# K and V pages loaded in runs of two rows into every second partition, and the sample softmax spread over several slots

## The reference

```python
def fox_sample(q, k, v, logf, k_past, v_past, logf_past):
    d_new = lax.cumsum(logf, axis=1).transpose(0, 2, 1)
    rev = (lax.cumsum(logf_past, axis=1, reverse=True) - logf_past).transpose(0, 2, 1)
    sp = jnp.einsum('bqhd,bkhd->bhqk', q, k_past) * scale
    sp = sp + d_new[:, :, :, None] + rev[:, :, None, :]
    ...
    p = jax.nn.softmax(jnp.concatenate([sp, sn], axis=-1), axis=-1)
    out = (jnp.einsum('bhqk,bkhd->bqhd', p[..., :n_past], v_past)
           + jnp.einsum('bhqk,bkhd->bqhd', p[..., n_past:], v))
```

## Time and profile before

| | |
|---|---|
| Median of 3 runs | 2012.65 us (2010.44 to 2016.42) |
| The profiled execution's own time | 2018.6 us |
| Its span, first to last instruction | 2016.9 us |
| Mean granted TensorE clock | 0.977 |
| PE, DVE, ACT, POOL busy over the span | 93%, 43%, 22%, 12% |
| Moved by DMA | 458.57 MB, 227 GB/s over the span |
| The slot loop | from about 70 us to 545 us |
| Idle time of POOL before `vpage` issues, ended by PE (L1290) | 233.6 us, 43 times |
| First matmul of the next stage (L1338) | 547.2 us |

### The profile page before, as it was taken

One profiled execution on the slowest core, in us unless ns is written; L12 is line 12 of the kernel. 1 busy time (PEld: TensorE's weight loads), 2 busy tenths in 40 slices (PEclk: granted clock), 3 DMA queues, 4 the chain that ended last, 5 costly groups with the idle time before them and its releaser, 6 DMA issues.

```text
span 2016.9 us, 33708 instructions
## 1 busy us (share of the span) xinstructions
PE 1876.5 (93%) x12473; PEld 1121.2 (56%) x12473; DVE 861.9 (43%) x1921; ACT 440.3 (22%) x1017; POOL 249.4 (12%) x381
## 2 busy tenths in 40 slices
PE   6999998888999999999999998987999999999994
PEld 4677655555488868888874487444333333333331
DVE  5644467777656523333344647245111111111115
ACT  3111124444301011101110305131222222212213
POOL 0203333333100000000000000000111111111110
PEclk9999999999999999999999999996999999999997
DMA  7859999999911140210121205344999999999966
GB/s 255 277 169 343 354 337 364 352 339 347 331 63 65 44 154 11 63 53 11 55 74 63 87 1 183 121 171 177 372 381 382 374 373 376 371 372 374 371 222 264
DMA packets 208164, 458.57 MB, mean 227 GB/s; under 512 B 18721, under 2 KB 47418, under 8 KB 207618
## 3 DMA queue, kind: packets, MB, share of 16 engines
q1 hardware_dynamic: 177554, 365.30, 50.8%
q0 software_dynamic: 30448, 91.13, 12.8%
HBM read 432.44 MB, written 32.17 MB: 230 GB/s over the span
## 4 chain that ended last, share of the span: by engine, by line
PE 82%; DVE 6%; ACT 4%; DMA 4%; issue 3%; DVEq 1%; SPq 0%; ACTq 0%; POOLq 0%; POOL 0%
PE ps L1338 20%; PE ps L1691 11%; PE ps L1722 6%; PE ps L1167 6%; PE ps L1403 6%; PE ps L1702 6%; PE ps L1432 5%; PE ps L1731 3%; PE ps L1182 3%; PE ps L1544 2%; PE ps L1290 2%; PE ps L1270 2%; PE ps L1148 1%; DVE kt L2230 1%; DMA vpage<-in_cache_v 1%
## 5 line engine op out<-in xcount | busy, mean ns | idle before, releaser
L1691 PE MATMUL ps<-gu,xgT 128*64 128x512 f32 x1024 | 228.7, 599 | 0.6 <-ACT xgT L2046 0.6
L1338 PE MATMUL ps<-xnT,ring 128*128 128x264 f32 x768 | 184.5, 392 | 3.2 <-ACT xnT L741 1.9
L2230 DVE STREAM_TRANSPOSE kt<-kraw 128x1024 f32<-128x1024 f32 x128 | 151.1, 1219 | 34.5 <-DMA kraw<-in_cache_k 25.3
L1338 PEld LDWEIGHTS ps<-xnT,ring 128*128 128x128 f32 x768 | 147.8, 193 | 30.5 <-ACT xnT L741 2.2
L876 POOL DMA_DIRECT2D vpage<-in_cache_v x228 | 122.4, 537 | 291.6 <-PE ps L1290 233.6
L3053 DVE TENSOR_TENSOR sig_a<-ps,sig_a 128x256 f32<-128x256 f32 x32 | 13.6, 425 | 322.9 <-ACT sig_a L2050 322.9
L1691 PEld LDWEIGHTS ps<-gu,xgT 128*64 128x64 f32 x1024 | 71.1, 138 | 133.0 <-issue 130.2
L1722 PE MATMUL ps<-wd,hidT_a 128*64 128x512 f32 x512 | 116.9, 598 | 20.2 <-ACT hidT_a L2056 11.2
L1702 PE MATMUL ps<-gu,xgT 128*32 128x512 f32 x1024 | 115.8, 592 | 0.0
L1167 PE MATMUL ps<-xnT,early 128*128 128x352 f32 x320 | 101.2, 472 | 4.4 <-DVE xnT L2174 4.4
L1167 PEld LDWEIGHTS ps<-xnT,early 128*128 128x128 f32 x320 | 60.6, 194 | 38.2 <-issue 8.7
(11 more groups left out here) (482 smaller groups left out, 2945.9 us busy)
## 6 DMA issues: line engine op xcount, KB each, us to landing
kraw<-in_cache_k SPq DMA_DIRECT2D x256, 256.0 KB, 5.3
wd<-in_w_expert_down SPq DMA_DIRECT2D x31, 2048.0 KB, 21.5
gu<-in_w_expert_gate SPq DMA_DIRECT2D x30, 2048.0 KB, 20.3
gu<-in_w_expert_up SPq DMA_DIRECT2D x30, 2048.0 KB, 25.1
vpage<-in_cache_v POOLq DMA_DIRECT2D x228, 256.0 KB, 5.8
ring<-in_w_in SPq DMA_DIRECT2D x12, 1024.0 KB, 8.1
yy<-y_d SPq DMA_DIRECT2D x16, 512.0 KB, 10.4
early<-in_w_in SPq DMA_DIRECT2D x6, 1024.0 KB, 11.7
```

The source lines that it names most:

```text
L1338: last = nc.tensor.matmul(bank(R.bank(name, f, q))[:, 0:QT], weight[:, k], src[:, k, cols], start=k == 0, stop=k == HK - 1)
L1691: last = nc.tensor.matmul(bank(0)[h * BA:(h + 1) * BA, :].rearrange("p (x n) -> p x n", x=2), src[:, k, 0:BA], weight[:, k, :, h * DE // 2 ...
L2230: nc.vector.transpose(kt[n % 2].rearrange("p c e s -> p (c e s)")[:, x * 1024:(x + 1) * 1024], kraw[n % 2].rearrange("p c d -> p (c d)")[: ...
```

## The change

- **Layout of a page.** Page p of a unit goes into the partitions of parity p % 2, two neighbouring rows of 512 floats to a partition (`page_rows`, `page_pairs`): 64 runs of 4 KB in place of 128 runs of 2 KB, for keys and values alike. The position of a token in a unit changes with it, so the order of `rev` changes too: partition p of `past` now holds pages 2p and 2p + 1, DVE writes the sum into a tile `paired` in the new order with four instructions in place of two, PE needs five small matmuls for `later` in place of two, and POOL stores `rev_d` in four DMAs of 64-float runs, without the wait behind them.
- **Joined maxima.** They move out of `join_scores` into `join_tops`, behind the prompt's pieces of the same slot.
- **Exponentials.** The first half of a sample is taken in slots with n % 8 = 0, the second half and the new tokens one slot later.
- **Turned probabilities.** Half a sample is turned in slots with n % 8 = 1 and the other half in slots with n % 8 = 3, both behind `turn_keys`; `st_ready` counts halves, and the load into place 5 waits for 16 of them. The first half waits for the values of the sample before only up to its fourth unit.
- **Queries.** `spread_queries` moves to slots with n % 8 = 4.

```diff
@@ -87,7 +87,7 @@
     c[:, C_ID:C_ID + P] = np.eye(P)
     c[:, C_CAUSAL:C_CAUSAL + P] = np.where(r[None, :] <= r[:, None], 0.0, NEG)
     c[:, C_BEFORE:C_BEFORE + P] = r[:, None] < r[None, :]
-    g, j = r // PAGES, r % PAGES
+    g, j = r // (PAGES // 2), r % (PAGES // 2)
     c[:, C_PAGES:C_PAGES + P] = (g[:, None] == g[None, :]) & (j[:, None] > j[None, :])
     hq, s = np.arange(QH), np.arange(NS)
     own = (s[None, None, :] // DS == np.arange(DB)[None, :, None]) & (s[None, None, :] % DS <= (hq % DS)[:, None, None])
@@ -241,6 +241,7 @@
         past = at("past", [P, 2, PAGE * H], w + 3 * 4096)
         after = at("after", [P, 2, H, PAGE], w + 5 * 4096)
+        paired = at("paired", [P, H, 4, 2, 16, 2], w)
         ptot = at("ptot", [P, 2, H], w + 7 * 4096)
         pgi = at("pgi", [P, 2], w + 7 * 4096 + 64, I32)
         early = [at(f"early{s}", [P, KD, 256], a_ring + s * 8192) for s in range(2)]
@@ -866,20 +867,27 @@
             elif place == 4:
                 R.read(eng, "sp", NSU - 1)
             elif place == 5:
-                eng.wait_ge(st_ready, DB)
+                eng.wait_ge(st_ready, 2 * DB)
+
+        def page_rows(place, p):
+
+            return place[p % 2::2, p // 2 * 2:p // 2 * 2 + 2, :]
+
+        def page_pairs(cache, page):
+
+            return cache[ds(page, 1)].rearrange("a (s j) d -> (a s) j d", j=2)
         def load_values(eng, n):
             numbers = unit_pages(eng, n)
             values_free(eng, n)
             for p, page in enumerate(numbers):
-                eng.dma_start(vpage[value_place(n)][:, p, :], t["cache_v"][ds(page, 1)].rearrange("a s d -> (a s) d")
+                eng.dma_start(page_rows(vpage[value_place(n)], p), page_pairs(t["cache_v"], page)
                               ).then_inc(v_in[value_place(n)], 16)
         def load_keys(eng, n, p, page):
-            eng.dma_start(kraw[n % 2][:, p, :], t["cache_k"][ds(page, 1)].rearrange("a s d -> (a s) d")
-                          ).then_inc(k_in[n % 2], 16)
+            eng.dma_start(page_rows(kraw[n % 2], p), page_pairs(t["cache_k"], page)).then_inc(k_in[n % 2], 16)
         def joined(i):
@@ -916,7 +924,7 @@
             with nc.allow_non_contiguous_dma("page numbers, one per partition"):
-                sp.dma_start(pgi, t["pages"].rearrange("a (g p) -> p (a g)", g=2)).then_inc(tables_in, 16)
+                sp.dma_start(pgi, t["pages"].rearrange("a (p g) -> p (a g)", g=2)).then_inc(tables_in, 16)
             sp.dma_start(convp, t["convp"]).then_inc(tables_in, 16)
@@ -958,7 +966,7 @@
                 load_unit(n)
                 if n == 3:
-                    sp.wait_ge(rev_stored, 16 * 8)
+                    sp.wait_ge(rev_stored, 16 * 4)
                     load_rev(0)
                 if n % SU == 6 and n < (DB - 1) * SU:
@@ -1193,8 +1201,13 @@
                     for g in range(2):
                         R.pe_free(pe, "later", g)
-                        nc.tensor.matmul(bank(R.bank("later", g))[:, 0:H], consts[:, C_PAGES:C_PAGES + P], ptot[:, g, :],
-                                         start=True, stop=True).then_inc(R.full, 1)
+                        for x in range(2):
+                            last = nc.tensor.matmul(bank(R.bank("later", g))[:, 0:H], consts[:, C_PAGES:C_PAGES + P],
+                                                    ptot[:, x, :], start=x == 0, stop=x == 1 and g == 1)
+                        if g == 0:
+                            last = nc.tensor.matmul(bank(R.bank("later", g))[:, 0:H], ident, ptot[:, 1, :],
+                                                    start=False, stop=True)
+                        last.then_inc(R.full, 1)
                 for x in MIX_TURNS[f]:
                     n_mix.pe_turn(pe, x)
             pe.wait_ge(early_k_in, 32)
@@ -1283,7 +1296,7 @@
                 pe.wait_ge(v_in[value_place(n)], 64 * values_in(n) + 64)
-                pe.wait_ge(st_ready, b + 1)
+                pe.wait_ge(st_ready, 2 * b + 1 + u // (SU // 2))
@@ -1885,13 +1898,14 @@
                     copy(("pt", k, p, g), probT[p][:, j0:j0 + nj, :],
                          lambda b: b[:, 0:nj * P].rearrange("p (j x) -> p j x", j=nj))
-            def exp_pages(b):
+            def exp_pages(b, r):
                 act.wait_ge(s_max, b + 1)
+                x = sprob[b % 2][:, r * 512:(r + 1) * 512]
+                nc.scalar.activation(x, x, ACT.Exp, bias=negmax[:, b:b + 1], accum_out=sums[:, b, r:r + 1]
+                                     ).then_inc(s_exp, 1)
+
+            def exp_new(b):
                 act.wait_ge(side_ready, SNEW_READY)
-                for r in range(2):
-                    x = sprob[b % 2][:, r * 512:(r + 1) * 512]
-                    nc.scalar.activation(x, x, ACT.Exp, bias=negmax[:, b:b + 1], accum_out=sums[:, b, r:r + 1]
-                                         ).then_inc(s_exp, 1)
                 nc.scalar.activation(pnew[b % 2], snew[:, b, :], ACT.Exp, bias=negmax[0:QH, b:b + 1],
                                      accum_out=sums[0:QH, b, 2:3]).then_inc(s_exp, 1)
@@ -1921,7 +1935,9 @@
                 if SU <= n < NSU + SU and n % SU == 0:
-                    exp_pages(n // SU - 1)
+                    exp_pages(n // SU - 1, 0)
+                if SU <= n < NSU + SU and n % SU == 1:
+                    exp_pages(n // SU - 1, 1), exp_new(n // SU - 1)
@@ -2205,8 +2221,11 @@
             for g in range(2):
                 R.made(dve, "later", g)
-                nc.vector.tensor_tensor(after[:, g], after[:, g], bank(R.bank("later", g))[:, 0:H].unsqueeze(2)
-                                        .to_broadcast([P, H, PAGE]), ALU.add)
+                for odd in range(2):
+                    nc.vector.tensor_tensor(paired[:, :, :, odd, :, g],
+                                            after[:, g].rearrange("p h (x s o) -> p h x s o", o=2, s=16)[:, :, :, :, odd],
+                                            bank(R.bank("later", g))[:, 0:H].unsqueeze(2).unsqueeze(3)
@@ -2345,23 +2364,27 @@
-                if u == SU - 1:
-                    dve.drain()
-                    for g in range(4):
-                        nc.vector.tensor_reduce(crest[:, g:g + 1], tops[g * QH:(g + 1) * QH, b, :], AX, ALU.max)
-                    dve.drain()
-                    for g in range(4):
-                        last = nc.vector.tensor_reduce(negmax[g * QH:(g + 1) * QH, b:b + 1], crest, AX, ALU.max, negate=True)
-                    last.then_inc(s_max, 1)
-
-            def turn_sample_probs(b):
-
-                dve.wait_ge(s_exp, 3 * b + 3)
+
+            def join_tops(b):
+
+                dve.drain()
+                for g in range(4):
+                    nc.vector.tensor_reduce(crest[:, g:g + 1], tops[g * QH:(g + 1) * QH, b, :], AX, ALU.max)
+                dve.drain()
+                for g in range(4):
+                    last = nc.vector.tensor_reduce(negmax[g * QH:(g + 1) * QH, b:b + 1], crest, AX, ALU.max, negate=True)
+                last.then_inc(s_max, 1)
+
+            def turn_sample_probs(b, r):
+
+                dve.wait_ge(s_exp, 3 * b + (1, 3)[r])
                 if b:
-                    dve.wait_ge(v_used, b * SU)
-                flat = sprobT.rearrange("p u x -> p (u x)")
-                nc.vector.transpose(flat, sprob[b % 2])
-                nc.vector.transpose(pnewT[b % 2], pnew[b % 2]).then_inc(st_ready, 1)
+                    dve.wait_ge(v_used, b * SU - (SU // 2, 0)[r])
+                half = slice(r * 512, (r + 1) * 512)
+                last = nc.vector.transpose(sprobT.rearrange("p u x -> p (u x)")[:, half], sprob[b % 2][:, half])
+                if r == 1:
+                    last = nc.vector.transpose(pnewT[b % 2], pnew[b % 2])
+                last.then_inc(st_ready, 1)
             def mask_own(b):
@@ -2375,8 +2398,6 @@
             for n in range(NSU + LAG):
                 if 0 < n <= NSU:
                     join_scores(n - 1)
-                if n % SU == 0 and n + SU < NSU:
-                    spread_queries(n // SU + 1)
                 if n == PROMPT0 - 1:
                     biased(0, 0)
                 if n == END:
@@ -2392,9 +2413,15 @@
                         invert_sums(k)
                 if n == 5:
                     take_new()
+                if 0 < n <= NSU and n % SU == 0:
+                    join_tops(n // SU - 1)
+                turn_keys(n + 2)
                 if SU < n < NSU + SU and n % SU == 1:
-                    turn_sample_probs(n // SU - 1)
-                turn_keys(n + 2)
+                    turn_sample_probs(n // SU - 1, 0)
+                if SU < n < NSU + SU and n % SU == 3:
+                    turn_sample_probs(n // SU - 1, 1)
+                if n % SU == 4 and n + SU < NSU:
+                    spread_queries(n // SU + 1)
                 if 2 * SU < n < NSU + LAG - 1 and n % SU == 1:
                     mask_own(n // SU - 2)
             near, far = slice(0, HT), slice(HT, NT)
@@ -3151,11 +3178,9 @@
```

(8 more changed lines are left out.)

1 line of the change is left out of this document (added).

## The result

| | before | after |
|---|---|---|
| Median, same chip | 2015.04 us (16 runs, 2009.81 to 2019.90) | 2022.14 us (16 runs, 2018.99 to 2033.83) |
| Ratio | | 1.0046, 95% interval 1.0034 to 1.0058 |
| Profiled execution: span, granted clock | 2016.9 us, 0.977 | 2031.4 us, 0.970 |
| First L1338 (after: L1351) | 547.21 us | 561.38 us |
| From L1294 (L1307) of the seventh sample to it | 29.7 us | 38.2 us |

A forecast was written before the change was run, and what follows sets the result against it. The prediction took the loop as bound by whichever of nearly full PE and DMA engines comes last in a slot. Terms -8.9, -6, -2, -3, +3, +0.9 sum to -16, taking median 2012.65 to 1997 us, range 1978 to 2010.

The forecast's parts named there:

- Rival 1 (DMA was the real bound): Slot loop: the DMA engines are the real bound; -31 us, or 1981 us; chance 0.20.
- Pages, -8.9: Slot loop: 4 KB runs end PE's direct waits on values and keys, -8.9 us, bounds -18.5 and 0.
- the price per piece: Page DMAs in the loop: 87.4 ns per 2 KB piece, 159.7 per 4 KB, so 18.5 us less of all engines.
- Rival 2: Slot loop: the 4 KB runs bring nothing, ends of samples give -8; -5 us, or 2007.5 us; chance 0.15.
- Rival 3 (dearer pieces): Pages in 64 partitions: new pieces cost more, deciding from 183 ns; +7 us, or 2020 us; chance 0.09.
- Maxima and exponentials, -6: Five sample ends: PE's 8.8 us of waits for turned prompt probabilities shrink, -6 us, bounds -8.8 and 0.
- a sign of being wrong: Slot loop: a new wait of ACT for the joined maxima would show the forecast wrong; no size given.
- Diagonal, -2: Slot loop: PE's 7.2 us of waits for the row sums' diagonal fall by 2 us, between 0 and -7.2.
- Clock, -3: Sample ends: shorter gaps bring back some of 8.1 us lost to low clock, -3 us, between 0 and -8.1.
- The end of the loop, +3 (0 to +9): Last half sample turned in slot 67, not 65, so place 5's load comes later; +3 us, 0 to +9.
- Start, +0.9: Before the slot loop: five small matmuls in place of two, without cover on PE, +0.9 us.
- rivals 2 and 4: In 4, the end of the loop eats the gain, +9 there; no change, 2012.6 us; chance 0.06.

The follow-up runs named there:

- Half pages: Kernel before, keys of units 2 to 63 and values of units 2 to 53 loading only rows 0 to 63 of each page: 2011.59 us, ratio 0.9985.
- layout only: Kernel before with the 4 KB page layout, new order of the sums and four rev_d stores alone: 2017.53 us, ratio 1.0016.
- the whole spread: Kernel before with the change's maxima, exponentials, turned probabilities and queries, old pages; with the last sample as before: 2013.52 us, ratio 0.9992.
- DVE's moves alone: Kernel before with only the maxima joined later and the queries spread in slots with n % 8 = 4: 2014.76 us, ratio 1.0006.
- The halves alone: Kernel before with only exponentials and turned probabilities in halves, keys ahead of them, last sample as before: 2010.45 us, ratio 0.9980.
- the two with the halves alone: Kernel before with exponentials and turned probabilities in halves, last sample as before: with old pages 2010.45 us (0.9980), with the 4 KB page layout 2008.68 us (0.9971).
- the spread alone: Kernel before with all of the change but the page layout and order of sums: 2021.54 us (1.0034); with the last sample whole 2013.52 us (0.9992).
- after, the same two ways: The changed kernel as it is, 2022.14 us (1.0046), and with the last sample's exponentials and turned probabilities whole as before, 2017.20 us (1.0012).

## Why the prediction was wrong

- **What bounds the kernel.** I wrote that the loop is bound by whichever comes last and then let the share of 0.98 argue for a DMA bound beside it. Half pages, with 36% fewer bytes and 0 to 0.3% less time, show that the chains of PE, ACT and DVE set the pace but for single places. *Rival 1 (DMA was the real bound) is refuted.*
- **Pages, -8.9: wrong, +3 measured (0 to +6) with the start's 0.7 in it.** Two steps failed. First, the price per piece went over all 308 DMAs; it holds at most on the hardware queue. Rival 2 noted the 3.3 KB packets of the software queue, and I should have taken the 160 DMAs of that queue out of the sum there: the earlier trace rows had told it. Second, "what the pages end directly" was taken as a gain: the pages landed only 0.1 to 0.3 us sooner and the waits on values stayed (8.2 us with the layout only), and even with half of the bytes gone the 8.0 + 0.9 us of waits gave only 3, while the diagonal's waits rose by 2.6. The Trainium skill, DMA: Bandwidth & Descriptors, section Rules for kernel authors, asks for 128 partitions. Here 64 partitions moved the same 346 GB/s and landed as soon, so no harm by it shows in this loop, though 0 to 0.3% of cost is not excluded. *Rival 3 (dearer pieces) is refuted*: 165 ns by the estimate, against its 183, and on the software queue no 4 KB piece appears at all. The 3 us stand without a place.
- **Maxima and exponentials, -6: right in the row, wrong in the sum.** 8.8 to 3.9 us, but the whole spread inside the loop gives a ratio of 0.9992, -1.6 us (-4.6 to +1.2). I had named a new wait of ACT as the upper bound and still took -6 where ACT's part was -5, "since DVE's comes on top". It doesn't: DVE's moves alone give nothing, and ACT now waits 4.5 us for the maxima, which the prediction had named as a sign of being wrong. The halves alone give about 4.
- **Diagonal, -2: wrong in sign.** 7.2 became 7.6 in after, and 7.0 to 14.1 in the other kernels with whole pages. DVE did get through its slots sooner, but then stood for keys, up to 5.46 us; only with half pages did the diagonal's waits fall with the spread, from 9.8 to 4.2.
- **Clock, -3: wrong in sign** in after (0.94 for 0.97); 0.94 to 0.97 in the kernels with the whole spread, 0.98 and 0.97 in the two with the halves alone. These are single profiles, and that of after is of a slow execution; over all executions the clock of the whole span is 0.9752 in after (0.970 to 0.979), 0.9794 in a kernel before, and 0.9801 with the halves alone. Where waits gave way to others the low clock went with them, as at 310 to 320 us.
- **The end of the loop, +3 (0 to +9): the mechanism right, the size wrong.** 8.5 us in the profiles, 5 to 8 in the medians, within the bounds of 0 to 9 but not near +3. The step that failed is "DVE will turn its half before that, so the load comes 0 to 9 us later", and "I take a third" of it: the turning stands last in slot 67, behind the prompt's pieces, and came at 534.42, after PE had begun its weighing of that slot at 533.53. `ring` came 11.6 us later. PE then waited for place 5 (1.59 us, the other sign of being wrong that the prediction had named), lost 2.8 us to the lower clock, and waited for the last values and for `xnT`. The DMA engines were near full before in this stretch, so what they idle is passed on for the most part; a third had no row behind it, and the clock was not in the term.
- **Start, +0.9: near.** 0.7 measured.
- **Which case it was:** rivals 2 and 4 together. I gave them 0.15 and 0.06 and let each keep a gain of the other's part; as one case, "the runs bring nothing, the ends give little and the end of the loop costs 8", they sum to slower.

## What to carry to other kernels

When work is moved out of a crowded slot for every sample, look at the last sample by itself: there the next stage's loads queue behind it, and an order that is neutral inside a loop can cost its full delay at the end. Take the queue apart before a price per piece is applied, and test a DMA bound by halving the bytes before anything is rebuilt to move them faster. A wait at a stage's end can cost more than itself, when the clock falls behind it. And when a wait of the critical engine goes, name what its supplier waits for next, here DVE for keys where it had waited for PE.

## What the runs showed of the hardware

- A busy share of 0.98 at 347 GB/s and of 0.84 at 223 GB/s in the same loop: the share falls far less than the bytes, and a packet of 1.8 to 1.9 KB on the hardware queue shows 118 ns where it showed 85.
- Contiguous runs of 2 or 4 KB make no difference to the software queue: 16,997 and 16,992 packets for 55.7 MB, 3.3 KB each, at 44.4 and 44.5%. On the hardware queue, in stretches where one transfer runs alone, a piece of 4 KB takes 159.7 ns and two of 2 KB take 174.8; in the loop the one takes 9.4 ns less than the two, about 165 ns by this estimate.
- After PE had stood 1.59 us, up to 543.28, the granted clock was 0.62 from 542 to 544 us and 0.50 from 544 to 548, and eight matmuls of 128x512 took 1.94 us where they take 1.07 at 1.00.
- Kernels that are the same program up to slot 64 reach the last weighing of the seventh sample at different times in their profiles: 516.54 and 513.36 us (the spread alone, with the last sample spread and whole), 523.20 and 513.25 (after, the same two ways). From the first matmul of the next stage to the end, where the fourteen kernels do not differ, the profiles take 1464 to 1471 us. So single profiles tell places and reasons here, and no times under some 10 us; over the executions of one kernel the time follows the granted clock (after: 2018.99 us at 0.979, 2033.05 at 0.970).
